# Prompt values stored by pairs of heads, and sample queries loaded once and copied on chip, in a hybrid encoder step

## The chip, the cores and the metric

The kernel runs on one core of a Trainium2 chip. The metric is device time in microseconds of one execution. Before the change it is 3593.35 us (median of 3 runs, 3592.12 to 3600.36).

## What is computed

One inference step of a hybrid encoder with two layers, in float32. There are 1024 prompt rows of one new stream and 8 running streams with 16 new frames each (128 sample rows), 1152 rows of width 1024 in all. Layer 0 mixes by two kinds of attention side by side: A, a sliding window, and B, differential attention with 4 heads (8 query and key heads of 64, 4 value heads of 128). Layer 1 mixes by C, a forgetting attention with 16 heads of 64. Each mixer is followed by a SwiGLU feed-forward of inner width 2816. The sample streams attend to caches of 2048 past rows each. Cut to what bears on the change:

```
qa, ka, va, qb, kb, vb = split(h @ w_in)              # layer 0: one projection for A and B
B:  p = softmax(q2 k2^T * scale, chunk mask)          # two score maps per head
    o = (p[:, 0] - lam * p[:, 1]) @ v                 # v: 4 heads of 128
C:  s = q k^T * scale + cq - ck, causal               # 16 heads of 64
    o = softmax(s) @ v
samples: the same with k, v = concat(cache (8, 2048, ...), the 16 new frames)
```

## The kernel before

The program is a row of stages, each with a barrier at its end: the first projection (`project_ab`, names abp_), A's attention for the prompt (pa_) and the samples (sa_), the joint attention of B (jb_), output projection (abm_), feed-forward (f_), the C projection (`project_c`, c_), the joint attention of C (jc_), output projection (cm_) and feed-forward again. All DMAs are issued by SyncE (SPq in the trace), in program order, on one queue.

The two projections go by pieces of output columns and, within a piece, by tiles of 128 rows. For each such step TensorE sums a product in PSUM, ScalarE copies it to one of two SBUF buffers z, and SyncE stores z to HBM: values go once to the kernel's output and once to an internal tensor (`v_ab`, `v_c`) that is laid out by rows, [1152 rows, width]. ScalarE may write z again two steps later, when its stores have landed (line 300 and line 614). The C projection cuts its 1024 value columns at 344 and 692.

The joint attention (`joint_attention`) works on the prompt and on the samples at the same time. It runs over units, one for each head of the prompt: 8 in jb, 16 in jc. A unit has 8 steps, one for each tile of 128 prompt queries, in the order 3, 4, 2, 5, 1, 6, 0, 7. Each engine has its program written out by hand, step by step, and they meet at semaphores. In a step n TensorE computes the scores of step n + 3 (lines 1489 to 1491), transposes the probabilities of n + 1 (line 1500) and, in every other step, multiplies them by the values (line 1517), or turns the last output back (line 1532). ScalarE computes the exponential of step n + 2 (line 1694), copies the output ahead of the turn back (line 1703) and copies transposed probabilities to SBUF (line 1659). VectorE takes the maxima and transposes the cache keys.

In the same unit one sample stream (and in jc one half of the heads) is worked off: its keys (`kc`, 4 MB, two buffers) are transposed, key scores are computed in step 7 (lines 1544 and 1552) out of four row groups of 32 partitions, and in the next unit ScalarE copies those scores (line 1714, step 0), exponentiates them (line 1727, steps 2 and 3) and TensorE multiplies by the cache values (`vc`, line 1607, steps 4 and 5). For this the queries of the samples must stand in each of the four row groups. One load, at lines 1371 to 1377, brings the queries of four units: SyncE issues four DMAs of the same 128 KB, one to each group of 32 partitions. It comes before unit 0 and then a unit ahead of units 4, 8 and 12 (4 in jb). VectorE waits for it in step 4 of the unit (line 1814) and spreads the unit's queries into `q_blocks` (line 1819).

The prompt's values are loaded per pair of heads (`load_v`, line 1322): 1024 rows by 128 columns to [128 partitions, 8 tiles, 128]. The source is laid out by rows, so each partition receives 8 separate pieces of 512 B. At a stage's start the order of SyncE is: planes of head 0 (`load_qk`), values of pair 0, keys of unit 0, queries, some small tensors, planes of head 1, values of pair 1, and then the loop at line 1395.

Of the kernel before, what the change touches and what calls it, by code (L numbers as in the profile page):

```python
# [25 lines left out]
P = 128  # L26
D = 1024
# [80 lines left out]
def project_ab(nc, name, x_tile, gain, w, tables, q_hi, q_lo, q_sample, v, k_rows_out, v_rows_out, direct):  # L108
# [14 lines left out]
    with Stage(nc, name) as st:  # L123
# [31 lines left out]
        def value_stores(s):  # L155
            c, t = steps[s]
            if AB_TURNED[c] == AB_PIECES[c][1]:
                return []
            src = z[:, s % 2, AB_TURNED[c]:AB_PIECES[c][1]]
            at = 0 if c == 0 else P  # L160
            return [(v[t * P:(t + 1) * P, at:at + AB_PIECES[c][1] - AB_TURNED[c]], src)] + v_rows_out(c, t, src)
# [285 lines left out]
def project_c(nc, name, ht_hi, ht_lo, w, bias, cache, q_hi, q_lo, q_sample, v, k_out, v_out, logf_prompt, logf_sample, ck, neg_c):  # L447
# [21 lines left out]
    with Stage(nc, name) as st:  # L469
# [29 lines left out]
        def row_stores(s):  # L499
            c, kind, t = steps[s]  # L500
            first, n, _ = C_PIECES[c]
            token = slice(t * P, (t + 1) * P)
            if kind == "k":
                return [(k_out(t)[:, first - D:first - D + n], z[:, s % 2, 0:n])]
            n = n_v if kind == "f" else n
            part = slice(first - 2 * D, first - 2 * D + n)
            return [(v[token, part], z[:, s % 2, 0:n]), (v_out(t)[:, part], z[:, s % 2, 0:n])]
# [644 lines left out]
def joint_attention(nc, name, groups, planes, k_first, v, v_cols, dv, q_sample, q_first, k_cache, v_cache, k_new, v_new,  # L1152
# [80 lines left out]
    with Stage(nc, name) as st:  # L1233
# [36 lines left out]
        out_ops = 1 if diff else 2  # L1270
# [34 lines left out]
        def _(sp):  # L1305
# [16 lines left out]
            def load_v(p):  # L1322
                if p >= 2:
                    sp.wait_ge(pv_done, S * (p - 1))
                c = v_cols(2 * p)
                sp.dma_start(vp[:, p % 2], v[0:PROMPT, c:c + P].rearrange("(t p) d -> p t d", p=P)).then_inc(
                    v_loaded[p % 2], 16)
# [43 lines left out]
            def load_q(g):  # L1371
                if g >= 1:
                    sp.wait_ge(q_done, 8 * g)
                first, streams = q_first + g // 2 * width, slice(g % 2 * P // 2, (g % 2 + 1) * P // 2)
                for a in range(4):
                    sp.dma_start(q_all[Q * a:Q * a + Q], q_sample[first:first + width, streams].rearrange(
                        "(j p) n -> p j n", p=Q)).then_inc(q_loaded, 16)
# [306 lines left out]
        def _(act):  # L1684
# [31 lines left out]

            def copy_new_scores(u):
# [19 lines left out]
            for u in range(U + 1):  # L1737
                for s in range(S):
# [22 lines left out]
                    if u >= 1 and s == 5:  # L1761
                        copy_probs(act, u - 1, 4)
                    if u < U and s == 5:
# [4 lines left out]
        def _(dve):  # L1768
# [43 lines left out]
            def blocks(u):  # L1812
                if u % 4 == 0:
                    dve.wait_ge(q_loaded, 64 * (u // 4 + 1))
# [937 lines left out]
def build(nc, a, out):  # L2752
# [3 lines left out]
    v_c = nc.dram_tensor("v_c", (TOKENS, D), F32, kind="Internal").ap()  # L2756
    planes_ab = nc.dram_tensor("planes_ab", (2, 13 * P, PROMPT), F32, kind="Internal").ap()
# [55 lines left out]
    project_ab(nc, "abp", x0, gain(0, 0), a["w_ab_in"][0], a["rope_table"], planes_ab[0], planes_ab[1], qs_ab, v_ab, k_rows_out, v_rows_out, direct)  # L2813
# [5 lines left out]
    joint_attention(nc, "jb", 1, planes_ab, D + P, v_ab, lambda h: P + h // 2 * P, P, qs_ab, 512,  # L2819
                    by_stream(a["cache_b_k"]), by_stream(a["cache_b_v"]), flat(out["b_k_sample"]), v_ab[samples, P:],  # L2820
                    o_ab, A_Q * DH, row_odd=a["odd_heads"], b_lambda=a["b_lambda"][0])
    with Stage(nc, "m0") as st:
# [6 lines left out]
        project_c(nc, "c", ht_hi, ht_lo, a["w_c_in"][0], a["c_forget_bias"], a["cache_c_logf"][0], planes_c[0], planes_c[1], qs_c, v_c,  # L2829
# [3 lines left out]
    joint_attention(nc, "jc", 2, planes_c, D, v_c, lambda h: h * DH, DH, qs_c, 0, by_stream(a["cache_c_k"]),  # L2833
# [40 lines left out]
```

## Time and profile before

| What | Value |
|---|---|
| Median of 3 runs | 3593.35 us |
| Profiled execution | 3596.04 us |
| Its span, first to last instruction | 3594.3 us |
| TensorE busy (matmul) | 3327.7 us, 93% |
| VectorE, ScalarE, GpSimd busy | 1598.0, 1124.3, 254.9 us |
| Mean granted TensorE clock | 0.966 |
| DMA | 493.16 MB, 398381 packets, 137 GB/s over the span |
| jb, from its first load to its last product | about 414 to 704 us |
| jc, the same | about 2055 to 2600 us |

The page's second part cuts the span into 40 slices. TensorE is at 9 tenths in most of them. The DMA engines are at 9 tenths in slices 6 and 7 (jb) and 24 to 29 (jc) and at 1 to 5 tenths nearly everywhere else, the feed-forwards at 1. The feed-forwards take most of the time and are not touched. So the stretches to look at are the two joint attentions, and the stores of the two projections.

### The profile page before, as it was taken

The numbers are of one execution on the slowest core, as the hardware profiler recorded it, in microseconds if no ns is written. First come the engines' busy times: TensorE is split into PE (matmuls) and PEld (weight loads), VectorE is DVE, ScalarE is ACT, GpSimd is POOL, SyncE is SP. The second block draws the span as 40 slices with busy tenths as digits, with TensorE's granted clock in tenths as the row PEclk, the third lists the DMA queues.
The fourth block names the chain that finished last, engine by engine and source line by source line (L and its number), as shares of the span: only waits on it lengthen the run. The fifth ranks groups of instructions, "written<-read, shape, count | busy, mean of one in ns | idle before, by whom it ended". The sixth has DMA issues, their size and how long they took to land. (4 is left out here: it accounts for less than half of the span.)

```text
span 3594.3 us, 62088 instructions
## 1 busy us (share of the span) xinstructions
PE 3327.7 (93%) x24520; PEld 2908.6 (81%) x24520; DVE 1598.0 (44%) x2913; ACT 1124.3 (31%) x2343; POOL 254.9 (7%) x338
## 2 busy tenths in 40 slices
PE   7997699798999999998799889999798999999997
PEld 7886477587999999997689866767577999999996
DVE  5427477463333333335331167777543333333334
ACT  4215355443212112112322155556433211121111
POOL 2310000032000000003000000000022000000003
PEclk9998799899999999999899999999999999999999
DMA  5436499533111111112554399999543111111112
GB/s 172 125 125 189 148 373 333 178 138 117 35 35 58 35 47 35 35 47 71 153 167 145 104 348 357 341 335 342 197 172 117 35 35 48 45 47 35 35 38 97
DMA packets 398381, 493.16 MB, mean 137 GB/s; under 512 B 68464, under 2 KB 250256, under 8 KB 398032
## 3 DMA queue, kind: packets, MB, share of 16 engines
q1 hardware_dynamic: 398176, 490.35, 41.2%
q8 instruction: 138, 2.26, 0.3%
q14 instruction: 67, 0.55, 0.0%
HBM read 407.10 MB, written 84.10 MB: 137 GB/s over the span
## 5 line engine op out<-in xcount | busy, mean ns | idle before, releaser
L2561 DVE TENSOR_TENSOR f_gated<-f_gated,f_up 128x384 f32<-128x384 f32 x132 | 73.1, 554 | 734.9 <-ACT f_gated L2491 734.9
L2585 DVE TENSOR_TENSOR f_y<-f_y,f_down 128x512 f32<-128x512 f32 x396 | 269.7, 687 | 229.4 <-PE f_down L2680 229.3
L2667 PE MATMUL f_gate<-m_ht_hi,f_w_hi 128*128 128x384 f32 x1056 | 355.0, 336 | 12.1 <-DVE f_w_lo L2612 12.1
L2667 PE MATMUL f_gate<-m_ht_lo,f_w_hi 128*128 128x384 f32 x1056 | 354.4, 336 | 0.0
L2667 PE MATMUL f_gate<-m_ht_hi,f_w_lo 128*128 128x384 f32 x1056 | 354.4, 336 | 0.0
L2667 PE MATMUL f_up<-m_ht_hi,f_w_lo 128*128 128x384 f32 x1056 | 352.7, 334 | 0.0
L2667 PE MATMUL f_up<-m_ht_hi,f_w_hi 128*128 128x384 f32 x1056 | 352.7, 334 | 0.0
L2667 PE MATMUL f_up<-m_ht_lo,f_w_hi 128*128 128x384 f32 x1056 | 352.7, 334 | 0.0
L2680 PE MATMUL f_down<-f_wo_hi,f_act_hi 128*128 128x512 f32 x792 | 313.4, 396 | 10.6 <-DVE f_y L2585 9.3
L2680 PE MATMUL f_down<-f_wo_hi,f_act_lo 128*128 128x512 f32 x792 | 309.9, 391 | 0.0
L2680 PE MATMUL f_down<-f_wo_lo,f_act_hi 128*128 128x512 f32 x792 | 309.6, 391 | 0.0
L2491 ACT ACTIVATE f_gated<-f_gate 128x384 f32<-128x384 f32 x132 | 65.0, 493 | 684.5 <-PE f_up L2667 684.3
L2667 PEld LDWEIGHTS f_gate<-m_ht_hi,f_w_hi 128*128 128x128 f32 x1056 | 199.5, 189 | 13.6 <-issue 12.8
L2667 PEld LDWEIGHTS f_gate<-m_ht_lo,f_w_hi 128*128 128x128 f32 x1056 | 199.5, 189 | 0.8
L2667 PEld LDWEIGHTS f_gate<-m_ht_hi,f_w_lo 128*128 128x128 f32 x1056 | 199.4, 189 | 0.0
L2667 PEld LDWEIGHTS f_up<-m_ht_hi,f_w_hi 128*128 128x128 f32 x1056 | 198.2, 188 | 0.0
L2667 PEld LDWEIGHTS f_up<-m_ht_lo,f_w_hi 128*128 128x128 f32 x1056 | 198.2, 188 | 0.0
L2667 PEld LDWEIGHTS f_up<-m_ht_hi,f_w_lo 128*128 128x128 f32 x1056 | 198.2, 188 | 0.0
L2680 PEld LDWEIGHTS f_down<-f_wo_hi,f_act_hi 128*128 128x128 f32 x792 | 149.5, 189 | 52.7 <-DVE f_y L2585 19.0
L1828 DVE STREAM_TRANSPOSE jc_kc<-jc_kc 128x512 f32<-128x512 f32 x256 | 180.8, 706 | 14.2
L2680 PEld LDWEIGHTS f_down<-f_wo_hi,f_act_lo 128*128 128x128 f32 x792 | 149.2, 188 | 31.8
L2680 PEld LDWEIGHTS f_down<-f_wo_lo,f_act_hi 128*128 128x128 f32 x792 | 149.5, 189 | 29.9
(404 smaller groups left out, 6756.6 us busy)
## 6 DMA issues: line engine op xcount, KB each, us to landing
jc_kc<-in_cache_c_k SPq DMA_DIRECT2D x64, 1024.0 KB, 11.1
jc_vc<-in_cache_c_v SPq DMA_DIRECT2D x64, 1024.0 KB, 10.3
jb_kc<-in_cache_b_k SPq DMA_DIRECT2D x32, 1024.0 KB, 11.7
jb_vc<-in_cache_b_v SPq DMA_DIRECT2D x32, 1024.0 KB, 8.6
m_raw<-in_w_ffn_in SPq DMA_DIRECT2D x44, 512.0 KB
f_raw<-in_w_ffn_in SPq DMA_DIRECT2D x44, 512.0 KB
f_raw_o<-in_w_ffn_out SPq DMA_DIRECT2D x22, 1024.0 KB, 6.2
m_raw<-x SPq DMA_DIRECT2D x18, 512.0 KB, 4.1
```

Of the source, the lines that this page charges most:

```text
L1828: dve.transpose(kc[:, u % 2, t, :], kc[:, u % 2, t + 1, :]).then_inc(kt_done, 1)
L2491: act.activation(silu[:, b], gate[:, q, 0:gw], ACT.Silu).then_inc(silu_done, 1)
L2561: dve.tensor_tensor(prod[:, b], silu[:, b], up[:, q, 0:gw], ALU.mult).then_inc(prod_done, 1)
L2585: dve.tensor_tensor(part, part, down[:, half, :], ALU.add).then_inc(added, 1)
L2667: last = pe.matmul(acc[:, q, 0:gw], a[:, s, k, u, :], b[:, k, token], start=(k == 0 and j == 0), stop=(k == KT - 1 and j == 2))
L2680: last = pe.matmul(down[:, half, :], a[:, s, t * P:(t + 1) * P], b[:, s, half * 512:(half + 1) * 512], start=(n == 0), stop=(n == 5))
```

## The change

Prompt values are also laid out by pairs: two new internal tensors, [pairs, 128 partitions, 8 tiles, 128], so that one load reads 4 KB in a row for each partition. In the first projection the store of B's prompt values goes there instead of to `v_ab`. In the C projection it goes there in place of `v_c`, cut where a pair of heads ends (at every 128 columns): the pieces of 344, 348 and 332 columns give 2, 3 and 2 stores. Sample rows still go to `v_ab` and `v_c`, and the stores to the kernel's outputs stay as they are.

The queries are loaded by one DMA, to partitions 0 to 31, and ScalarE copies them three times, to partitions 32, 64 and 96. These copies, with their wait for the load, stand in ScalarE's program in step 1 of units 0, 4, 8 and 12 (0 and 4 in jb), behind that step's copy of transposed probabilities. VectorE waits in step 4 for the three copies.

```diff
@@ project_ab, value_stores
             src = z[:, s % 2, AB_TURNED[c]:AB_PIECES[c][1]]
+            if AB_PIECES[c][0] == VB and t < TILES_P:
+                return [(v_pairs[:, :, t].rearrange("h p d -> p h d"), src.rearrange("p (h d) -> p h d", d=P))] + v_rows_out(c, t, src)
             at = 0 if c == 0 else P
@@ project_c, row_stores
-            return [(v[token, part], z[:, s % 2, 0:n]), (v_out(t)[:, part], z[:, s % 2, 0:n])]
+            out = [(v_out(t)[:, part], z[:, s % 2, 0:n])]
+            if t == TILES_P:
+                return [(v[token, part], z[:, s % 2, 0:n])] + out
+            stores, a = [], part.start
+            while a < part.stop:
+                heads = max(1, (part.stop - a) // P) if a % P == 0 else 1
+                b = min(a - a % P + heads * P, part.stop)
+                src = z[:, s % 2, a - part.start:b - part.start].rearrange("p (h d) -> p h d", h=heads)
+                stores.append((v_pairs[a // P:a // P + heads, :, t, a % P:a % P + (b - a) // heads].rearrange("h p d -> p h d"), src))
+                a = b
+            return stores + out
@@ joint_attention, SyncE
-                c = v_cols(2 * p)
-                sp.dma_start(vp[:, p % 2], v[0:PROMPT, c:c + P].rearrange("(t p) d -> p t d", p=P)).then_inc(
-                    v_loaded[p % 2], 16)
+                sp.dma_start(vp[:, p % 2], v_pairs[p]).then_inc(v_loaded[p % 2], 16)
-                for a in range(4):
-                    sp.dma_start(q_all[Q * a:Q * a + Q], q_sample[first:first + width, streams].rearrange(
-                        "(j p) n -> p j n", p=Q)).then_inc(q_loaded, 16)
+                sp.dma_start(q_all[0:Q], q_sample[first:first + width, streams].rearrange("(j p) n -> p j n", p=Q)).then_inc(q_loaded, 16)
@@ joint_attention, ScalarE
+            def copy_queries(g):
+                act.wait_ge(q_loaded, 16 * (g + 1))
+                for a in range(1, 4):
+                    act.activation(q_all[Q * a:Q * a + Q], q_all[0:Q], ACT.Copy).then_inc(q_copied, 1)
                     if u >= 1 and s == 5:
                         copy_probs(act, u - 1, 4)
+                    if u < U and u % 4 == 0 and s == 1:
+                        copy_queries(u // 4)
@@ joint_attention, VectorE
-                    dve.wait_ge(q_loaded, 64 * (u // 4 + 1))
+                    dve.wait_ge(q_copied, 3 * (u // 4 + 1))
@@ build
+    v_pairs_ab, v_pairs_c = (nc.dram_tensor(n, (heads, P, TILES_P, P), F32, kind="Internal").ap()
+                             for n, heads in (("v_pairs_ab", B_H), ("v_pairs_c", C_H // 2)))
```

## Rows read from the trace of the kernel before

**Rows 1.** Windows: stretch, us, busy us per engine (x instructions), PEclk, DMA, GB/s.

```profile
2110.00:2560.00 450.00, 429.08 (x6520) 314.39 (x6516) 328.58 (x741) 269.04 (x660) 0.00 (x0) 1.00 0.97 339
```

**Rows 2.** Waits, 413 to 703: who waited, releaser, total us, times, longest.

```profile
PE jb_scores_a L1489 <- DMA jb_q_lo<-planes_ab: 14.6, 2, 11.2
```

**Rows 3.** Timeline, jc opening: start us, us, engine, operation, [idle before, releaser].

```profile
2066.69 9.94 SPq L1376 DMA_DIRECT2D jc_q_all<-qs_c  x4
...
2073.55 0.50 ACT L1659 ACTIVATE jc_probs_t<-jc_turned 128x384 f32<-128x384 f32 x1
...
2074.55 0.39 ACT L1703 ACTIVATE jc_o_turn<-jc_pv 128x256 f32<-128x256 f32 x1
...
2076.09 0.56 PE L1532 MATMUL jc_pv<-jc_halves,jc_o_turn 128*128 128x64 f32 x4
...
2086.53 0.62 SPq L1320 DMA_DIRECT2D jc_k_hi<-ck  x1
...
2090.92 0.79 PE L1489 MATMUL jc_scores_a<-jc_k_both,jc_q_hi 128*128 128x512 f32 x1 [8.63 <-DMA jc_k_hi<-ck]
```

**Rows 4.** Windows, jc opening.

```profile
2077.00:2080.00 3.00, 1.56 (x15) 1.08 (x14) 2.83 (x8) 1.69 (x6) 0.00 (x0) 1.00 1.29 187
...
2081.00:2084.50 3.50, 1.29 (x13) 1.15 (x11) 0.00 (x0) 0.98 (x2) 0.00 (x0) 1.00 0.17 37
...
2091.00:2096.00 5.00, 5.00 (x54) 3.73 (x54) 4.27 (x9) 1.15 (x4) 0.00 (x0) 0.50 1.06 376
```

**Rows 5.** Timeline, jb opening.

```profile
427.01 7.48 SPq L1376 DMA_DIRECT2D jb_q_all<-qs_ab  x4
...
431.96 0.38 ACT L1703 ACTIVATE jb_o_turn<-jb_pv 128x256 f32<-128x256 f32 x1 [0.76 <-PE jb_pv L1517]
```

**Rows 6.** ScalarE groups by form: operation, shapes, count, busy us, mean ns.

```profile
L2482 ACT ACTIVATE f_w_hi<-m_raw 128x2048 fp32r<-128x2048 f32 x20 | 38.0, 1900 | 0.0
...
L1727 ACT ACTIVATE jc_s_scores<-jc_s_scores,jc_s_neg 128x1024 f32<-128x1024 f32 x16 | 18.4, 1150 | 1.7 <-DVE jc_s_neg L1849 1.7
```

**Rows 7.** Timeline, jc, the unit that uses the third query load.

```profile
2333.78 0.43 ACT L1703 ACTIVATE jc_o_turn<-jc_pv 128x256 f32<-128x256 f32 x1
...
2334.85 0.87 ACT L1659 ACTIVATE jc_probs_t<-jc_turned 128x512 f32<-128x512 f32 x2 [0.64 <-PE jc_turned L1500]
...
2334.81 0.56 PE L1532 MATMUL jc_pv<-jc_halves,jc_o_turn 128*128 128x64 f32 x4
...
2340.90 0.66 PE L1532 MATMUL jc_pv<-jc_halves,jc_o_turn 128*128 128x64 f32 x4 [0.61 <-ACT jc_o_turn L1703]
```

**Rows 8.** Line 1544, four per unit, four windows: ns, first and last start.

```profile
L1544 PEld LDWEIGHTS jc_turned<-jc_bias,jc_select x64: 181/182/184, 2101.0 to 2573.4; 32*128 32x128 f32 x64
...
L1544 PEld LDWEIGHTS jc_turned<-jc_bias,jc_select x12: 181/182/184, 2194.6 to 2260.1; 32*128 32x128 f32 x12
...
L1544 PEld LDWEIGHTS jc_turned<-jc_bias,jc_select x12: 181/182/184, 2260.0 to 2321.4; 32*128 32x128 f32 x12
...
L1544 PEld LDWEIGHTS jc_turned<-jc_bias,jc_select x8: 181/182/184, 2321.3 to 2355.3; 32*128 32x128 f32 x8
```

**Rows 9.** Windows, jc: inside a query load; ahead of two key scores.

```profile
2185.50:2191.50 6.00, 6.00 (x133) 4.76 (x127) 3.52 (x8) 2.57 (x9) 0.00 (x0) 1.00 1.08 173
...
2255.00:2261.00 6.00, 6.00 (x69) 4.21 (x59) 4.50 (x12) 3.35 (x8) 0.00 (x0) 1.00 0.68 222
...
2316.00:2322.00 6.00, 6.00 (x81) 4.53 (x70) 4.29 (x11) 3.37 (x9) 0.00 (x0) 1.00 0.92 323
```

**Rows 10.** Timeline, jc: inside the key scores of unit 7.

```profile
2326.76 0.58 PE L1552 MATMUL jc_s_ps<-jc_kc,jc_q_blocks 32*32 32x512 f32 x1 [1.16 <-issue]
```

**Rows 11.** The C projection: timeline of SyncE, then waits.

```profile
1735.82 12.18 SPq L560 DMA_DIRECT2D c_zeros<-in_cache_c_logf  x8
...
PE c_acc L753 <- ACT c_z L619: 4.5, 1, 4.5
...
SPq L566 <- ACT c_z L619: 103.6, 41, 4.8
```

More of the change, by code:

```diff
@@ L105, with project_ab @@
 AB_KEYS = (KA, KB)
-def project_ab(nc, name, x_tile, gain, w, tables, q_hi, q_lo, q_sample, v, k_rows_out, v_rows_out, direct):
+def project_ab(nc, name, x_tile, gain, w, tables, q_hi, q_lo, q_sample, v, v_pairs, k_rows_out, v_rows_out, direct):
     slots = 3
@@ L444, with project_c @@
             (0, 512, "q"), (512, 512, "q"))
-def project_c(nc, name, ht_hi, ht_lo, w, bias, cache, q_hi, q_lo, q_sample, v, k_out, v_out, logf_prompt, logf_sample, ck, neg_c):
+def project_c(nc, name, ht_hi, ht_lo, w, bias, cache, q_hi, q_lo, q_sample, v, v_pairs, k_out, v_out, logf_prompt, logf_sample, ck, neg_c):
     gw = TOKENS // 3
@@ L1149, in strided, with joint_attention @@
     return bass.AP(ap.tensor, ap.offset + offset, [list(ap.ap[0])] + [list(d) for d in dims])
-def joint_attention(nc, name, groups, planes, k_first, v, v_cols, dv, q_sample, q_first, k_cache, v_cache, k_new, v_new,
+def joint_attention(nc, name, groups, planes, k_first, v_pairs, dv, q_sample, q_first, k_cache, v_cache, k_new, v_new,
                     o, o_first, ck=None, neg_c=None, row_mask=None, selector=None, row_odd=None, b_lambda=None):
@@ L1269, in joint_attention @@
              "s_inv_done", "s_pv_done", "scaled", "ot_done", "ot_copied", "s_stored"))
-        out_ops = 1 if diff else 2
+        out_ops, q_copied = 1 if diff else 2, st.sem("q_copied")
         emptied_sem = {"act": act_emptied, "dve": dve_emptied}
@@ L2811, in v_rows_out @@
         return new_frames("a_v_sample", src) if t == TILES_P else []
-    project_ab(nc, "abp", x0, gain(0, 0), a["w_ab_in"][0], a["rope_table"], planes_ab[0], planes_ab[1], qs_ab, v_ab, k_rows_out, v_rows_out, direct)
+    project_ab(nc, "abp", x0, gain(0, 0), a["w_ab_in"][0], a["rope_table"], planes_ab[0], planes_ab[1], qs_ab, v_ab, v_pairs_ab, k_rows_out, v_rows_out, direct)
     prompt_attention(nc, "pa", A_Q // 2, lambda i, e: (2 * i + e) * DH, lambda i, e: D + (i // 2) * DH,
@@ L2818, in build @@
                   v_ab[samples, 0:P], a["a_sinks"], o_ab)
-    joint_attention(nc, "jb", 1, planes_ab, D + P, v_ab, lambda h: P + h // 2 * P, P, qs_ab, 512,
+    joint_attention(nc, "jb", 1, planes_ab, D + P, v_pairs_ab, P, qs_ab, 512,
                     by_stream(a["cache_b_k"]), by_stream(a["cache_b_v"]), flat(out["b_k_sample"]), v_ab[samples, P:],
@@ L2828, in build @@
                      lambda t: x2[t * P:(t + 1) * P], gain_next=gain(1, 0))
-        project_c(nc, "c", ht_hi, ht_lo, a["w_c_in"][0], a["c_forget_bias"], a["cache_c_logf"][0], planes_c[0], planes_c[1], qs_c, v_c,
+        project_c(nc, "c", ht_hi, ht_lo, a["w_c_in"][0], a["c_forget_bias"], a["cache_c_logf"][0], planes_c[0], planes_c[1], qs_c, v_c, v_pairs_c,
                   tile_of(flat(out["c_k_prompt"]), flat(out["c_k_sample"])),
@@ L2832, in build @@
                   out["c_logf_sample"][0].rearrange("s f h -> (s f) h"), ck, neg_c)
-    joint_attention(nc, "jc", 2, planes_c, D, v_c, lambda h: h * DH, DH, qs_c, 0, by_stream(a["cache_c_k"]),
+    joint_attention(nc, "jc", 2, planes_c, D, v_pairs_c, DH, qs_c, 0, by_stream(a["cache_c_k"]),
                     by_stream(a["cache_c_v"]), flat(out["c_k_sample"]), v_c[samples], o_c, 0, ck=ck, neg_c=neg_c,
```

## The prediction

> **What bounds the kernel now.** I read the page's busy shares and slices first, then the table of windows by stage, then the waits and timelines of the two joint attentions (jb for layer 0, jc for layer 1), the only stages that the new loads and copies touch. In the middle of jc TensorE is busy 429 of 450 us and the DMA engines are at 0.97 [rows 1]: two limits side by side, with ScalarE at 60%. TensorE is hardly ever seen waiting for data there. The times at which the key scores open tell more: 472.3 us over 15 units, 31.5 each, against 30.65 in the two units that no query load touches (2260.0 to 2321.3) [rows 8]. So 472.3 - 15 x 30.65 = 12.5 us is all that the steady part of jc could give back without a shorter instruction list. Both openings do wait for DMA: TensorE stands 8.63 us before head 1 in jc [rows 3], and in jb 14.6 - 11.2 = 3.4 us [rows 2].
>
> **The change, part by part.**
>
> (a) *Queries loaded once.* A load today is four issues of 128 KB in pieces of 64 numbers (256 B): 2048 pieces, tomorrow 512. In jc's opening the four hold SyncE 9.94 us [rows 3], the DMA engines move 187 GB/s while they drain, then 37 GB/s, because SyncE had been held and reaches the second head's planes late [rows 4]. The last of those is issued at 2086.53 and TensorE restarts at 2090.92 [rows 3]. Three quarters of the query bytes gone and SyncE free some 7.5 us earlier puts head 1 in SBUF by about 2083, ahead of need, so this stall goes. What is late next is (b).
>
> (b) *The wait moves to ScalarE, and three steps earlier.* Today VectorE waits for the queries in step 4 of unit 0. Now ScalarE waits for them in step 1, behind the copy at 2073.55 [rows 3]. The queries are queued behind the 4 MB of keys, which drain until about 2077 (the low-bandwidth stretch begins there [rows 4]). With the cheaper value load ahead I put the landing at 2078. Then three copies, each 32 partitions x 1024 numbers. The trace has no such instruction: half of a 128 x 2048 copy is 0.95 us, an exponential of 128 x 1024 is 1.15 [rows 6], so 2.85 to 3.45 for three; I take 3.0, nearer to the copy. Queued behind them on ScalarE are the exponential of step 2 and the copy of the first output, done today at 2074.94 [rows 3]; it would be done at 2078 + 3.0 + 0.5 + 0.4 = 2081.9. TensorE's turn-back waits for it, and everything that ScalarE empties after. The turn-back starts today at 2076.09 [rows 3], so it shifts 5.8 us, and the work that ends today where the stall begins, at 2090.92 - 8.63 = 2082.3, ends at 2088.1. Against 2090.92 that is 2.8 us won of the 8.6. TensorE's clock row reads 0.50 (1.2 GHz) in the five us after the old stall [rows 4]; a pause of 5.8 us in place of 8.6 may bring the same fall, but over work that is paced by ScalarE. I take 3.5 us won in jc's opening; the ends are 8 won (the stall goes and the copies lie beside it) and 1 lost.
>
> In jb the same sum is worse, since only 3.4 us of stall are there to trade. SyncE's four held issues end at 434.49 [rows 5], a sign of when the keys ahead have drained, and I take 434.8 for the landing. The output copy, at 431.96 + 0.38 today [rows 5], would end at 434.8 + 3.0 + 0.9 = 438.7, 6.4 us later. TensorE comes late for that copy anyway, in jc by 1.2 us (2076.09 against 2074.94); of that I count 0.7, which leaves 5.7. TensorE reaches head 1 some 2.3 us later than today. Its half clock after the old stall may move ahead of the restart as well. I take 0.5 lost, ends 4 lost and 3 won. Both openings together: 3.0 won.
>
> (c) *Copies in the running pipeline.* Four more groups of queries come in mid-stream: jb's second, jc's second to fourth. Their loads are issued a unit ahead, so ScalarE finds the data there. But step 1 lies in its densest stretch: in jc's unit 8 the output copy starts at 2333.78 and ends 0.6 us before TensorE uses it (2334.81), one gap of 0.64 us follows, and then ScalarE runs without a break until TensorE waits 0.61 us for it at 2340.90 [rows 7]. So 3.0 us put in front of 2333.78 are covered for about 0.7 and delay TensorE by 2.3. Four times: 9.2 us lost. Ends: 4 x 0.7 = 3 if TensorE's instruction gaps swallow part, 4 x 3.4 = 14 if nothing covers.
>
> (d) *DMA time given back.* Inside a query load the DMA engines move 173 GB/s [rows 9] against 339 in the whole stretch [rows 1], so 512 KB and what is between it take 5 to 7 us in place of about 1.5. TensorE doesn't wait for these bytes. What I see instead: in the 6 us ahead of the key scores the DMA share is 0.68 in a clean unit and 0.92 in the unit after a query load [rows 9], and inside that unit's key scores TensorE stands 1.16 us for "issue", that is for no semaphore [rows 10]. The units at the two loads take 65.4 us for two and 33.9 for one, against 30.65: 4.1 and 3.25 us over [rows 8]. I read that as instructions fetched late through DMA engines that have lost their pause. If the loads shrink to a quarter, most of the 12.5 us should come back; I take 9 in jc and 0.5 in jb, ends 0 and 13. The Trainium skill speaks against this reading: "Runtime: NRT & Kernel Launch", section on instruction fetch mechanics, calls the crossing of a 16 KiB block mostly hidden. By that rule nothing comes back here and the sum would be 9.5 us higher; the 1.16 us row stands against it, and I make the case a rival.
>
> (e) *Values by pairs.* Each load of 512 KB goes from 1024 pieces of 512 B to 128 of 4 KB. It is never waited for in either stage after the opening. Its saving is part of (a) and (d).
>
> (f) *The stores.* In the first projection one store of 256 KB becomes one of four times the pieces, beside matmuls that leave SyncE idle between steps: nothing. In the C projection prompt rows are stored in 2, 2 and 3 pieces where there was 1 (the pieces are cut at 344 and 692): 32 more issues of about 0.35 us on SyncE. They matter only at the start, where SyncE is held 12.18 us by the cache loads and TensorE already waits 4.5 us for ScalarE's z, whose buffer waits for its stores [rows 11]. Two steps' stores, one issue more each: 0.7 us lost, ends 0 and 2. If SyncE's idle time in the later steps were gone, 24 issues x 0.35 = 8 us would be the price; but it waits 103.6 us for z in 41 steps, 2.5 in each [rows 11], and the extra stores take at most 0.7 of them.
>
> **Sum** against the profiled execution, 3596.04 us (span 3594.3): -3.0 + 9.2 - 9.5 + 0.7 = -2.6, so 3593.4. That execution lies 2.7 us above the median of the runs, 3593.35; against the median the forecast is 3591 us. Copies on ScalarE and DMA time given back nearly cancel. A measurement of this kernel can tell about 0.3% (10.8 us) from no change.
>
> **The rivals.**
>
> *Relief that is hidden anyway.* The issue gaps have another cause and stay. For it: TensorE has waits of "issue" in clean units too. Against: they are longest after query loads. Then -3.0 + 9.2 + 0.7 = +6.9 over the median: 3600.
>
> *ScalarE's wait decides (slower).* The openings win nothing, because ScalarE stands behind 4 MB of keys in both, and each mid-stream group costs its full copies. Price: openings 4 lost, 4 x 3.0 = 12, C projection 0.7, 3 returned by DMA: +14, so 3607. It decides once the queries land later than about 2081 in jc. For it: [rows 7]; against: TensorE has nothing to do but wait from 2082 today. The Trainium skill's advice to issue a DMA early and wait late ("DMA: Bandwidth & Descriptors", rules for kernel authors) points the same way, as the change waits earlier.
>
> *The transfers are the bound (faster).* The DMA engines, at 0.97, set jc's pace more than TensorE's rows show. Everything of the 12.5 comes back, the openings give 8 in jc and 1 in jb, and the copies cost 4 x 1.5 = 6 since a unit freed of late data has room: -12.5 - 9 + 6 + 0.7 = -15, so 3578.
>
> **How the numbers follow.** Forecast (near-cancelling, 3585 to 3597) 0.48; hidden relief 0.20; ScalarE decides 0.14; transfers decide 0.18. Faster by over 0.3% is most of the last and a little of the first: 0.17. Slower is most of ScalarE's case: 0.13. Same: 0.70. The ends of the terms added in full would be -29 and +21; eight in ten I put between 3577 and 3607.
>
> **What would show it.** In the changed profile: 18 ScalarE copies of about 1.0 us from the query tile, and six query issues in place of 24; in jc's opening a ScalarE wait of about 4 us for the queries and no TensorE wait for the head's planes, key scores of unit 0 opening near 2097.5 (today 2101.0 [rows 8]); units without a query load still at 30.6 us, those with copies near 32 to 33, issue gaps in key scores mostly gone. Wrong would be: a ScalarE copy far from 1 us, units at 30.6 with copies in them (ScalarE had room), or clean units that get shorter (DMA was the bound).

## Result: 3615.73 us, 0.5% slower

| | before | after |
|---|---|---|
| Median of 10 runs each | 3594.42 us (3591.24 to 3604.80) | 3615.73 us (3610.15 to 3618.81) |
| Ratio, 95% interval | 1 | 1.0050 (1.0040 to 1.0061) |
| Span of the profiled execution | 3594.3 us | 3613.7 us |

The forecast was 3591, its range ended at 3607. The change costs 21 us, and the 19.4 us by which the two spans differ lie almost wholly in jb and jc. "Opening" is from a stage's first instruction to the first key score of its first unit, "steady" from there to the key scores of its last unit, "tail" the rest; all are read from starts and ends in the traces:

| us | before | after | difference |
|---|---|---|---|
| jb opening / steady / tail | 41.9 / 222.4 / 23.7 | 47.0 / 226.2 / 25.2 | +5.1 / +3.8 / +1.5 |
| jc opening / steady / tail | 46.9 / 472.3 / 23.7 | 49.3 / 478.8 / 25.9 | +2.4 / +6.5 / +2.2 |
| C projection | 324.3 | 325.1 | +0.8 |

The remaining -2.9 us are in stages that the change doesn't touch, or hardly. The tails are chance as far as the traces tell: over the seventeen of this study they lie between 22.3 and 25.9 us in jb and jc, with copies and without. An "issue gap" is a stop of TensorE for which the profile shows no semaphore.

In the steady part of jc the three units that hold copies take 34.1, 34.1 and 35.6 us. In the profile of before the same units took 33.0, 33.9 and 33.3, but issue gaps had made them slow; in a second profile of that kernel (e11, below) they took 30.6, 30.6 and 32.1. Against that one, each group costs 3.5 us. Unit 0 loses another 3.6 (34.3 us against 30.7) to an issue gap of 2.1 us and a fall of the clock behind it. This seems to come with the change, though no step of the prediction has it: the gap stands in nine of the ten kernels that load a stage's first queries once (not in e8), with unit 0 at 33.4 to 34.3 us, and in none of the four with an unshifted list that load them four times (before, e1, e7, e11), with unit 0 at 30.6 to 30.7. Why it comes is not shown, nor that it moves the medians: e8 without it and e9 with it are alike there.

**The middle of jc.** A window of the changed kernel, shifted by the 9.1 us by which its jc starts later; columns as in [rows 1]:

```profile
2119.00:2569.00 450.00, 426.75 (x6473) 312.97 (x6471) 323.07 (x729) 273.02 (x654) 0.00 (x0) 0.98 0.92 328
```

Against [rows 1] the DMA share fell from 0.97 to 0.92, as the change meant. But the trace holds 47 matmuls less in the same 450 us, and its mean clock is 0.98 in place of 1.00. The transfers were relieved and the stage got slower. That they weren't its limit is shown by e7 below, which takes bytes away and changes nothing else.

**The opening of jc.** Timeline of the changed kernel, the rows that answer to [rows 3]:

```profile
2075.88 2.43 SPq L1385 DMA_DIRECT2D jc_q_all<-qs_c  x1
...
2081.64 0.50 ACT L1667 ACTIVATE jc_probs_t<-jc_turned 128x384 f32<-128x384 f32 x1
...
2087.31 0.61 SPq L1332 DMA_DIRECT2D jc_k_hi<-ck  x1
...
2090.39 3.21 ACT L1728 ACTIVATE jc_q_all<-jc_q_all 32x1024 f32<-32x1024 f32 x3 [8.25 <-DMA jc_q_all<-qs_c]
2093.62 0.47 ACT L1702 ACTIVATE jc_probs<-jc_scores_a,jc_neg_top 128x256 f32<-128x256 f32 x1
...
2094.09 0.37 ACT L1711 ACTIVATE jc_o_turn<-jc_pv 128x256 f32<-128x256 f32 x1
...
2094.51 1.11 PE L1540 MATMUL jc_pv<-jc_halves,jc_o_turn 128*128 128x64 f32 x4 [10.18 <-ACT jc_o_turn L1711]
```

ScalarE has nothing to do from 2082.1 to 2090.4: it stands in front of the first copy until the queries land. Three copies take 3.21 us. The exponential and the output copy behind them were wanted at 2084, and TensorE stands 10.18 us. The stall before head 1 [rows 3] is gone; in its place is a longer one, beginning 20.1 us behind the stage's start where the old one began at 27.2. SyncE did what was expected of it: head 1's last plane is issued at 2087.31, in the clock of before 2078.2, 8.3 us earlier.

**The opening of jb**, the same, to be held against [rows 2, 5]:

```profile
433.29 3.21 ACT L1728 ACTIVATE jb_q_all<-jb_q_all 32x1024 f32<-32x1024 f32 x3 [6.46 <-DMA jb_q_all<-qs_ab]
...
437.42 0.69 PE L1537 MATMUL jb_pv<-jb_ident,jb_o_turn 128*128 128x128 f32 x2 [7.86 <-ACT jb_o_turn L1711]
```

**A group in mid-stream.** Timeline, then two windows just before and behind TensorE's restart; they answer to [rows 7]:

```profile
2209.75 0.38 ACT L1711 ACTIVATE jc_o_turn<-jc_pv 128x256 f32<-128x256 f32 x1
2215.15 1.09 ACT L1722 ACTIVATE jc_s_scores<-jc_turned 128x512 f32<-128x512 f32 x2 [5.02 <-PE jc_turned L1560]
...
2219.70 3.21 ACT L1728 ACTIVATE jc_q_all<-jc_q_all 32x1024 f32<-32x1024 f32 x3
...
2223.83 0.66 PE L1540 MATMUL jc_pv<-jc_halves,jc_o_turn 128*128 128x64 f32 x4 [2.67 <-ACT jc_o_turn L1711]
```

```profile
2222.50:2225.60 3.10, 1.64 (x14) 1.34 (x15) 1.08 (x4) 3.07 (x9) 0.00 (x0) 1.00 1.05 390
2225.80:2229.00 3.20, 3.20 (x17) 2.74 (x15) 1.49 (x4) 2.91 (x7) 0.00 (x0) 0.50 1.05 387
```

TensorE waits 2.67 us where it waited 0.61, and right behind that pause its granted clock reads 0.50 (1.2 GHz) for one stretch of 3.41 us, with no further pause in it. All four mid-stream groups show both (2.67 us three times in jc, 2.25 in jb). In the kernel before no stretch at 1.2 GHz lies between the first and the last key scores of either stage. Note also the second row: 4.5 us ahead of the copies ScalarE had been idle for 5.02 us. The waits of the stage, before and then after:

```profile
PE jc_pv L1532 <- ACT jc_o_turn L1703: 9.0, 15, 0.6
PE jc_s_ps L1552 <- issue: 4.6, 4, 1.7
```

```profile
PE jc_pv L1540 <- ACT jc_o_turn L1711: 15.2, 15, 2.7
PE jc_s_ps L1560 <- issue: 2.6, 3, 1.1
PE jc_s_ps L1597 <- issue: 2.1, 1, 2.1
```

### The profile page after: what moved, and what is told of

Its sections match the earlier page's. It is cut to its first block and busy times, and to the rows that moved or that the text cites. A ratio compares the mean times of both kernels' runs of the same rounds, so it can differ in the third digit from the quotient of the medians.

```text
span 3613.7 us, 62120 instructions
## 1 busy us (share of the span) xinstructions
PE 3335.1 (92%) x24520; PEld 2914.5 (81%) x24520; DVE 1598.1 (44%) x2913; ACT 1143.6 (32%) x2361; POOL 254.5 (7%) x338
```

## The experiments

Theory A after the traces: ScalarE's place decides, by its wait for the queries in the openings and by its copies in mid-stream with the half clock behind each. Rivals: the values' larger pieces make other loads late (B), the opening alone (D) or the mid-stream alone (E) decides. Ratios are to the kernel before, run alongside.

**e1_values_only, e2_queries_only.** The change in its two halves. e1 is the changed kernel with `load_q` and VectorE's wait as before; e2 the kernel before with

```
-for a in range(4): sp.dma_start(q_all[Q * a:Q * a + Q], ...)
+sp.dma_start(q_all[0:Q], ...)
+copy_queries(u // 4)          # ScalarE, step 1 of each fourth unit
```

> Only the values part of the change: stored and loaded by pairs of heads; each group of queries is loaded four times, as before. Theory A (ScalarE's work and wait is what costs: openings +7.4 us, copies in mid-stream, and the half clock that follows each pause) expects the whole loss to be gone: 3590 to 3597 us, openings of jb and jc at 42 and 47 us from the stage's start to the first key score, 3.41 us half-clock stretches in mid-stream gone. Rival B (the values' 4 KB pieces crowd out the keys' and queries' pieces on the DMA engines, so that these land later) expects openings still 3 to 7 us longer than before and 3600 to 3608 us. Rival C (DMA time given back is real): a few us below before, 3585 to 3590.

> Only the queries part: loaded once, copied by ScalarE in step 1; values stored and loaded as before. Theory A expects all of the loss or a little more, 3613 to 3620 us: ScalarE waits 6 to 8 us for the first queries in each opening, TensorE 2.7 us at each mid-stream copy. Rival B expects less than half of the loss, 3596 to 3605, with the queries landing some us earlier than in the changed kernel.

e1: 3595.15, ratio 0.9998 (0.9989 to 1.0006); openings 40.8 and 47.4. e2: 3614.89, ratio 1.0048 (1.0036 to 1.0060). The queries' part is the whole loss; the values' part costs and wins nothing, to within 4 us. B falls.

**e3_first_only.** The changed kernel; groups after each stage's first are loaded four times:

```
 def load_q(g):
+    if g == 0: one load, return
+    for a in range(4): four loads
-if u < U and u % 4 == 0 and s == 1:
+if u == 0 and s == 1:
     copy_queries(u // 4)
```

> The changed kernel, but only the first group of queries of each stage is loaded once and copied by ScalarE; the later groups (one in jb, three in jc) are loaded four times. It splits the loss. Theory A by the trace: the openings' 7.4 us stay, and most of the slower units' 10.3 us (3.8 in jb, 6.5 in jc) go: 3604 to 3608 us, with no TensorE wait of 2.7 us and no half-clock stretch in mid-stream except those that unit 0 itself brings. Rival D (the opening alone decides, since a late start leaves the load queue late through the whole stage): 3611 to 3616, with slow units all the same. Rival E (mid-stream copies decide): 3594 to 3600.

3606.63, ratio 1.0026 (1.0015 to 1.0037): half the loss is back. Openings 46.4 and 49.3 as in the changed kernel, and no TensorE wait for ScalarE of 2.67 us in mid-stream. D and E fall: there are two losses, by the ratios 9.3 us at the first groups and 8.6 at the later ones, the second net of what one load in place of four gives.

**e4_on_gpsimd.** The copies on an idle engine:

```
+for g in range(U // 4):                      # GpSimd
+    pool.wait_ge(q_loaded, 16 * (g + 1))
+    for a in range(1, 4):
        ...                                   # wait for its own copy before
        pool.tensor_copy(q_all[Q * a:Q * a + Q], q_all[0:Q]).then_inc(q_copied, 1)
-copy_queries(u // 4)                         # ScalarE
```

> The changed kernel with the 18 copies on GpSimd, idle in the middle of both stages, each group as soon as its load has landed; ScalarE waits for nothing new. Theory A expects both losses gone: openings at 42 and 47 us or less, 3588 to 3597 us. If GpSimd's copies take far longer than ScalarE's 1.05 us (3 us each would still fit before VectorE's step 4 of unit 0 in jc only just), VectorE and then TensorE wait in the openings: 3597 to 3604. Rival F (the loss is not ScalarE's but the late landing of a single query load): VectorE's wait at step 4 moves the openings as now, 3605 to 3615.

3591.91, ratio 0.9987 (0.9979 to 0.9996). Openings 38.7 and 43.5, 3.2 and 3.4 us shorter than before the change. Two rows of its timeline:

```profile
2077.82 3.22 POOL L1474 COPY jc_q_all<-jc_q_all 32x1024 f32<-32x1024 f32 x3 [19.04 <-DMA jc_q_all<-qs_c]
...
2083.05 0.79 PE L1504 MATMUL jc_scores_a<-jc_k_both,jc_q_hi 128*128 128x512 f32 x1 [4.64 <-DMA jc_k_hi<-ck]
```

The queries land 26.0 us behind jc's start (2051.8), as late as in the changed kernel (26.2), and now nobody but GpSimd waits. The stall before head 1 is 4.64 us in place of 8.63: the relief of step (a), seen by itself. The last rival of the expectation falls.

**e5_queries_first.** The wait taken away by an earlier load, the copies left in step 1:

```
 load_qk(0)
+load_q(0)
 load_v(0)
 load_keys(0)
-load_q(0)
```

> The changed kernel with the first query load issued by SyncE right after head 0's planes, ahead of the values and the 4 MB of keys; ScalarE still makes the three copies in step 1, and the mid-stream copies stay. If the wait is what costs in the openings (theory A), ScalarE waits for nothing there, what is left is 3.2 us of copies: the openings (stage start to the first key score of the first unit) come out near 32 us in jb and 37 in jc, against 36.6 and 40.1 in the changed kernel and 28.4 and 34.0 with the copies on GpSimd; 3605 to 3610 us in all. If the copies themselves cost as much as the wait, the openings stay within 2 us of the changed kernel's: 3612 to 3617. The keys land 0.5 us later at most.

3605.58, ratio 1.0023 (1.0013 to 1.0034), 10 us better than the changed kernel. Openings 39.6 and 43.0, level with GpSimd's 38.7 and 43.5. (The expectation's numbers for openings end at TensorE's first use of the query blocks, for the new keys; in that reading e5 has 29.1 and 33.8.) Timeline, jc:

```profile
2078.00 3.22 ACT L1728 ACTIVATE jc_q_all<-jc_q_all 32x1024 f32<-32x1024 f32 x3
...
2082.13 0.66 PE L1540 MATMUL jc_pv<-jc_halves,jc_o_turn 128*128 128x64 f32 x4 [1.95 <-ACT jc_o_turn L1711]
...
2090.58 0.50 PE L1497 MATMUL jc_scores_a<-jc_k_both,jc_q_hi 128*128 128x512 f32 x1 [3.48 <-DMA jc_k_hi<-ck]
```

No idle time ahead of the copies. They still hold TensorE 1.95 us, but head 1's planes are late anyway (3.48 us), so in jc's opening the copies are nearly free and only the wait was dear (43.0 against 43.5 with GpSimd's copies; 39.6 against 38.7 in jb).

**e6_first_and_split.** As e5, one copy in each of steps 1, 2 and 3: `if u % 4 == 0 and s in (1, 2, 3): copy_queries(u // 4, s)`.

> As the kernel with the first queries loaded first, and the three copies of every group spread over steps 1, 2 and 3, one in each. If what costs in mid-stream is one pause of 2.7 us and the 3.41 us at 1.2 GHz that follow it, three delays of 1.07 us, each half covered by slack of 0.6 to 0.7 us in ScalarE's row, leave TensorE waits of at most 1.1 us, no half clock in mid-stream, and units with copies at 31 to 32 us: 3593 to 3600 us. If ScalarE's total work is what costs, all of 3.2 us per group stays: 3602 to 3608.

3600.94, ratio 1.0014 (1.0005 to 1.0023): between the two expectations, and the reason of neither holds. The copy in step 1 is nearly covered (TensorE waits 0.51 us), those in front of the step-2 output are not (2.19 us), and the fall of the clock followed in three of the four groups. In jc the copy unit without the fall takes 2.9 us more than in e9 below (33.5 against 30.6), the two with it 4.5 and 4.1 more. Cutting the copies up only spreads them over a stretch in which ScalarE has too little slack for them.

**e7_no_later_queries.** The kernel before without `load_q` for every group after a stage's first: it leaves out reading the later queries and uses the first ones again.

> The kernel before without the query loads after the first group of each stage (jb's second, jc's second to fourth): it leaves out reading these queries, and uses the first ones again. It measures step (d) of the prediction by itself, in full: what the stream would win if no query byte moved in it. If the issue gaps come from DMA engines that the query loads keep busy: 9 to 12.5 us in jc, 3584 to 3588 us, and TensorE's waits of over 1 us for no semaphore, 177 us and 399 us behind jc's start, gone. If they have another cause (hidden relief): 3592 to 3596 us, and the same waits at the same places of the instruction list.

3594.08, ratio 0.9997 (0.9988 to 1.0007). The rival "hidden relief" holds: all later query bytes together are worth 1 us by the ratio, at most 4 by its interval. The issue gaps are still there. A row of the kernel before, then one of e7:

```profile
2233.39 0.58 PE L1552 MATMUL jc_s_ps<-jc_kc,jc_q_blocks 32*32 32x512 f32 x1 [1.29 <-issue]
```

```profile
2225.84 0.58 PE L1550 MATMUL jc_s_ps<-jc_kc,jc_q_blocks 32*32 32x512 f32 x1 [1.56 <-issue]
```

Counted in matmuls and weight loads from jc's first, both are at the 4269th.

**e8_gpsimd_first.** e4 with e5's order of loads.

> The kernel with the copies on GpSimd, and the first query load issued ahead of the values and keys. With the copies on GpSimd the queries are needed only by VectorE in step 4, and TensorE waited 1.31 us for the query blocks in jb's opening and nothing in jc's. Theory A: at most 1.3 us better than the 3592 of that kernel, 3588 to 3593. Rival (keys come later by what the 512 small pieces take, and the planes of head 1 with them): 3592 to 3596.

3590.52, ratio 0.9984 (0.9975 to 0.9993): the best of the study, not to be told from e4.

**e9_in_idle.** e5 with the mid-stream copies one step earlier, still on ScalarE, still in one piece:

```
+if 4 <= u < U and u % 4 == 0 and s == 0:
+    copy_queries(u // 4)
 if u >= 1 and s == 0:
     copy_scores(u - 1, 0)      # waits for TensorE's key scores
```

> The kernel with the first queries loaded first, and the mid-stream copies on ScalarE one step earlier: in step 0, right ahead of the copy of the key scores, where ScalarE stands idle 5.0 us in every unit waiting for TensorE. The same three copies by the same engine, 3.2 us in one piece, nothing else changed. If where they stand decides (theory A), the 15 us between e5_queries_first (3605.6) and e8_gpsimd_first (3590.5) come back, with no TensorE wait of 2.67 us and no half clock in mid-stream: 3589 to 3594. If the loss is in having them on ScalarE at all, or in the writes to the query tile while TensorE and VectorE run: 3600 to 3606.

3590.74, ratio 0.9987 (0.9978 to 0.9996). Timeline and the stage's waits:

```profile
2193.57 3.22 ACT L1728 ACTIVATE jc_q_all<-jc_q_all 32x1024 f32<-32x1024 f32 x3
2198.56 0.60 ACT L1722 ACTIVATE jc_s_scores<-jc_turned 128x512 f32<-128x512 f32 x1 [1.77 <-PE jc_turned L1560]
```

```profile
PE jc_pv L1540 <- ACT jc_o_turn L1711: 9.0, 15, 0.6
```

The idle time of 5.02 us has become 3.22 of copies and 1.77 of idle time, and TensorE's waits for ScalarE are back at 9.0 us, as before the change. The same work one step earlier is worth 15 us by the medians. In the traces the four units with copies take 3.5, 3.3, 3.0 (jc) and 3.3 us (jb) less than in e5, 13.1 together. In jc 2.0 of each is TensorE's shorter wait; the other 1.0 to 1.5 us are matmuls that no longer run at 1.2 GHz. That is the price of one fall, a little under half of its 3.41 us.

**e10_two_copies.** e5 with two copies in place of three in the mid-stream groups (`for a in range(1, 4 if g == 0 else 3)`): it leaves out the fourth row group's new queries.

> The kernel with the first queries loaded first and copies in step 1, with two copies instead of three in the four mid-stream groups: the fourth row group keeps old queries, which leaves out part of the computation. It separates the clock from the wait. TensorE's wait falls by one copy, 1.05 us, from 2.67 to 1.6 us. If the wait alone costs, 4 x 1.05 = 4.2 us are won over e5_queries_first's 3605.6: 3601 to 3602. If the shorter pause no longer brings the 3.41 us stretch at 1.2 GHz (half of 3.41 us each), 4 x 2.75 = 11 us: 3594 to 3595. If some of the stretches stay, in between.

3597.31, ratio 1.0004 (0.9995 to 1.0012), 8.3 us below e5 by the medians and 6.8 by the ratios, each of which is known to about 3 us only; the waits alone would give 4.2. Timeline, then windows behind the three pauses in jc:

```profile
2209.03 0.66 PE L1540 MATMUL jc_pv<-jc_halves,jc_o_turn 128*128 128x64 f32 x4 [1.59 <-ACT jc_o_turn L1711]
```

```profile
2209.20:2213.00 3.80, 3.66 (x32) 3.07 (x33) 2.76 (x7) 3.80 (x9) 0.00 (x0) 1.00 1.05 388
2335.60:2339.00 3.40, 3.26 (x30) 2.73 (x30) 2.77 (x7) 3.40 (x7) 0.00 (x0) 1.00 1.05 388
2463.90:2467.00 3.10, 3.10 (x18) 1.87 (x17) 2.81 (x7) 3.10 (x6) 0.00 (x0) 0.50 1.04 384
```

After a pause of 1.59 us the clock stayed up twice in jc and also in jb (1.17 us there), and fell once. The medians alone would not part the clock from the wait, the units do: against e5 the two of jc where it stayed up are 1.9 and 1.8 us shorter and jb's 2.7, the one where it fell 1.2, about the missing copy's 1.05. The fall is a cost of its own.

**e12_planes_up.** e8 with `load_qk(1)` right behind `load_keys(0)`.

> The kernel with GpSimd's copies and the first queries loaded first, and head 1's planes issued right behind the keys, ahead of the frame mask, the head rows, the bias and the new keys, whose issue holds SyncE some 9 us. TensorE's stall for these planes in jc's opening was 8.63 us before the change and 2.96 with GpSimd's copies. If SyncE's held issue is what makes them late, the stall goes, with part of the 10.2 us at 1.2 GHz behind it: 3 to 6 us won, 3585 to 3588. If the keys' 4 MB decide, the planes land as now: 3589 to 3592. If bias or new keys become late for the first key scores: 3592 to 3598.

3596.81, ratio 1.0002 (0.9993 to 1.0011): 6 us worse than e8, as the last of the three outcomes had it. The stall before head 1 went only from 2.96 to 2.30 us, and VectorE now waits 6.2 us for the new keys, whose issue has moved behind the planes; TensorE waits for VectorE's blocks in turn. Waits, 2078 to 2099:

```profile
DVE jc_turned_new L1849 <- DMA jc_new<-out_c_k_sample: 6.2, 1, 6.2
PE jc_turned L1584 <- DVE jc_q_blocks L1834: 5.7, 1, 5.7
```

**e11_shifted_list, e13_shift_by_matmuls, e14_shift_250, e15_shift_64.** What the issue gaps are: the kernel before, with instructions added at the head of TensorE's list in jc. One run each.

```
+pe.nop()                                                       # e11: 128 times
+pe.wait_ge(setup, 5)                                           # e13, e14, e15
+pe.matmul(scores_a[:, 0:P], ident_b[:], mask[:], ...)          # e13: 64 times
+pe.matmul(scores_a[:, 0:16], ident_b[:], mask[:, 0:16], ...)   # e14: 125, e15: 32 times
```

> The kernel before with 128 empty instructions at the head of TensorE's list in jc, where it waits for its first planes anyway. It asks what the issue gaps of step (d) are. In four kernels with four different amounts of query traffic TensorE stood 1.1 to 1.8 us for no semaphore 174 to 180 us and 394 to 400 us behind jc's start, always in the key scores. If these are places of the instruction list (its fetch), all move to earlier lines by 128 instructions, some 4 to 5 us, out of or to another part of the key scores, and other gaps move as well. If they are times at which the DMA engines are busiest, or belong to the key scores' own work, they stay at the same lines and times.

> The kernel before with 64 small matmuls at the head of TensorE's list in jc, from about 2057 on, while it waits for its first planes (their result is overwritten): 128 instructions, and these are executed ones, since the 128 empty instructions of e11_shifted_list left no mark in the trace and were perhaps never in the program. The question is the same. If the issue gaps of over 0.7 us in the key scores are places of the instruction list, they move 128 instructions ahead: those that stood at the 4269th, 8007th and 10747th TensorE instruction of jc in all kernels stand at the same count with the new ones counted, that is on other work. If they belong to this work, they stay on it, at the 4397th, 8135th and 10875th. In time no change that one run can tell: 3590 to 3602.

> The kernel before with 125 small matmuls (250 TensorE instructions) at the head of jc's list. In e13_shift_by_matmuls (128 instructions) the issue gaps left their places: counted with the new instructions they stand at 2528, 3527, 5268, 6266, 9006, 10004, 11745, which is again 249 times a whole number apart from each other, and the steady part took 486.4 us (475 to 481 in the kernels with the same stream and no ScalarE copies in step 1). If TensorE's list comes in blocks of some 249 matmuls and weight loads, a shift by 250 puts the same work at the block ends again: gaps of over 0.7 us at 1530, 4269, 8007 and 10747 plus 250, the steady part back at 475 to 481 us. If e13's gaps were this one run's luck, the gaps stand anywhere else.

> The same with 32 matmuls, 64 instructions. By blocks of 249: the gaps stand at places that are a multiple of 249 (within 3) behind 1530, counted with the new instructions, and on other work than before; the steady part somewhere between 475 and 490 us. If not blocks: gaps at 1594, 4333, 8071 and 10811, on the same work as before.

e11 (3590.83) decides nothing on its question: its page counts 62088 instructions, as before the change, so the empty ones are not among those that ran. It is a second profile of the kernel before instead, and as that it is worth much: its steady part of jc takes 466.3 us, not 472.3 (first and last starts 2102.1 and 2568.4 against [rows 8]):

```profile
L1548 PEld LDWEIGHTS jc_turned<-jc_bias,jc_select x64: 181/182/184, 2102.1 to 2568.4; 32*128 32x128 f32 x64
```

e13, e14 and e15 took 3604.20, 3605.54 and 3602.68 us beside 3605.06 for the kernel before, no difference that one run tells. The executed instructions did move the gaps. Places of TensorE's waits of over 0.4 us for no semaphore, from the 1000th to the 14000th matmul or weight load of jc, added ones counted (in brackets the us):

| kernel | places |
|---|---|
| before | 1530 (0.46), 3767 (0.46), 4017 (1.59), 4269 (1.29), 7009 (1.16), 7503 (1.05), 8007 (0.43), 9498 (0.49), 10747 (1.69) |
| e11 (the same program) | 1530 (0.46), 4269 (1.56), 8007 (0.97), 9498 (0.49), 10747 (0.87) |
| e7 | 1530 (0.73), 4269 (1.56), 7009 (0.61), 7503 (1.32), 8007 (0.70), 10747 (1.15) |
| e4 | 1027 (1.71), 1530 (0.67), 4269 (1.56), 8007 (0.97), 9498 (0.49), 10747 (1.15) |
| e13 (128 added) | 2528 (1.59), 3023 (0.88), 3527 (1.40), 5268 (0.89), 6266 (0.74), 9006 (1.54), 10004 (0.76), 11745 (0.66), 12242 (2.12), 12744 (0.74) |
| e14 (250 added) | 1283 (1.30), 4525 (1.63), 7265 (1.40), 7759 (0.84), 8263 (0.64), 9754 (0.49), 10501 (1.53), 11003 (1.45) |
| e15 (64 added) | 2024 (0.75), 2528 (0.70), 5268 (1.14), 8007 (1.86), 9006 (0.57), 11243 (1.70), 11745 (0.48) |

(4017 stands behind a wait for ScalarE that had ended 0.57 us before.) The distances between them are multiples of 249.2 to within 7 (4269 - 1530 = 2739, eleven times 249.0; 3527 - 2528 = 999, four times 249.8). e13 and e15 share four places though their work is shifted by another amount, and e14's are those of before and e4 plus 256 (all but 10501), on work six instructions away. So a gap belongs to a place in the list. Most show inside the key scores, where a matmul or weight load starts every few hundredths of a us:

```profile
2169.75 0.61 PE L1557 MATMUL jc_s_ps<-jc_kc,jc_q_blocks 32*32 32x512 f32 x2 [1.59 <-issue]
```

```profile
2237.84 0.58 PE L1557 MATMUL jc_turned<-jc_kc,jc_q_blocks 32*32 32x512 f32 x1 [1.63 <-issue]
```

(e13's 2528th and e14's 4525th.)

The traces also hold what ends these stops. On the page of before a queue of its own carries instructions, 138 packets of 16384 bytes; the second line is the window 2231.0 to 2231.1 us, which holds one of them:

```profile
q8 instruction: 138, 2.26, 0.3%
q8 instruction: 1, 0.02, 68.4%
```

That packet starts at 2231.01 and takes 1.1 us, and TensorE goes on at 2233.39 (the row in e7's section), 2.4 us behind its start. Over all seventeen traces, in the same part of jc, each of the 102 stops of over 0.4 us for no semaphore ends 2.3 to 2.8 us behind the start of such a packet. Of the 248 stops that a semaphore ended, 4 do (4017 is one); the others end anywhere from 0.3 to 12 us behind one. So TensorE stands at these places for a block of instructions that comes late. Why a block is late at one crossing and not at the next is not shown.

The Trainium skill, "Runtime: NRT & Kernel Launch", section on instruction fetch mechanics, gives blocks of 256 instructions; with the waits that lie between the matmuls the 249 fit it, while "mostly hidden" holds only for most of the crossings: these show 0.4 to 2.1 us each. e14 contradicts its own expectation in one point: its steady part took 475.6 us, not the 466 to 472 of this measure in the unshifted kernels, with a gap at 10501 that has no counterpart in the unshifted kernels. One execution each does not tell what an alignment is worth.

## Why the prediction was wrong

Medians: 3615.7 - 3591 = 24.7 us too low. Point by point, by its own steps:

**(a) SyncE free earlier: right.** 8.3 us earlier against 7.5 foretold. With the copies out of ScalarE's way (e4, e8) the two openings are 6.6 and 5.6 us shorter together than before the change; "the stall goes" was too much, 4.64 and 2.96 us of it stay there.

**(b) The wait moved to ScalarE: the step that failed first.** The landing was put at 2078 in jc, since the keys were thought to drain until 2077, where a stretch of low bandwidth begins [rows 4]. It came at 2090.39 - 9.1 = 2081.3, just beyond the point of 2081 that the text itself gave for "ScalarE's wait decides". In jb it was 436.4 in the clock of before, against 434.8. The trace of before had the answer: of the keys' last load in jc, issued at 2065.62, it says (1 MB, us to landing)

```profile
jc_kc<-in_cache_c_k SPq DMA_DIRECT2D x1, 1024.0 KB, 14.4
```

so the keys landed at 2080.0, and the DMA engines were at a share of 1.29 in that stretch of low bandwidth [rows 4], busy to the end. In the changed kernel the keys landed at 2080.5 in the clock of before, the queries right behind them.

Predicted for both openings -3.0, measured +7.5 in the traces. Of these 10.5 us, 3.3 and 1.6 are the later landings. Another 2.5 were never in the step's own sum: it gives 2.8 us won in jc and 2.3 lost in jb, and 3.5 won and 0.5 lost were taken, for a half clock that would cost less. It cost more: the clock reads 0.50 for 13.65 us in each changed opening, against 10.24 before in jc and 6.83 in jb. And TensorE now waits 1.4 us in jc and 1.6 in jb for VectorE's query blocks, since VectorE gets the queries after ScalarE; the prediction had nothing for this, and in the kernel before there is no such wait. e5 shows that it is the wait: with the data there, the same three copies in the same place leave the openings within 1 us of GpSimd's. Their price, 3.21 against 3.0, was right.

**(c) Copies in mid-stream: the mechanism right, the term too small.** TensorE waits 2.67 - 0.61 = 2.06 us more per group in jc (2.3 foretold). What was left out is the half clock behind the pause: half of 3.41 is 1.7 us. 2.06 + 1.7 = 3.8, four times 15; e5 against e8 and e9 measures 15.1 and 14.8. The units in the traces say a little less, 3.0 to 3.5 each. The prediction did weigh the clock in the openings and forgot it here.

**(d) DMA time given back: wrong.** 9.5 us were foretold; e7, with no later query byte at all, returns 1.1 (loses 2.5 to wins 4.3). Half of the reading of [rows 10] holds: the stop of 1.16 us ends 2.4 us behind the start of an instruction packet, so these were instructions fetched late. The other half, that the query loads make them late, fails: the gaps sit at places of the list whether or not queries are loaded, so "hidden relief" was the right case. By the Trainium skill's sentence that the step set against itself nothing comes back, and by e7 nothing did that shows. The 12.5 us over the clean units [rows 8] were partly the one execution profiled: e11 runs the same program 6 us faster through the same stretch. Traffic may add to single gaps; that is not shown, since e11, with all of the traffic, lacks the same four as e4 does (3767, 4017, 7009, 7503).

**(e), (f) Right.** Values by pairs: e1's 0.9998. C projection: +0.8 us in the trace against 0.7, but between the traces of kernels without the new stores the stage varies by over 2 us, so this shows only that nothing large was missed. Two slips of the text change nothing here: the pieces store in 2, 3 and 2 parts, not 2, 2 and 3, and the favourable ends of the terms add up to -21, not -29 (-8 - 3 + 3 - 13).

**What would have shown it.** Of the signs listed, the 18 copies of 1.05 us and the missing wait for the head's planes came; the ScalarE wait was 8.25 us, not 4, units with copies took 34.1 to 35.6 us in jc, not 32 to 33, and the issue gaps stayed. Not foreseen at all: the gap and the half clock in unit 0, 3.6 us in the trace.

Errors: (b) 10.5, (c) 5.8, (d) 8.4, together 24.7. Each is known to 2 or 3 us only, they mix single traces with medians, and unit 0's 3.6 us stand in none of them, so that the sum fits to the tenth is luck. They had one sign, which the near-cancelling sum had hidden. Of the rivals, "ScalarE's wait decides" had place and mechanism; its +14 lacked the clock and gave 3 us back to DMA.

**The version that beats both.** Queries loaded once, first group issued ahead of the keys, copies on GpSimd (e8, 0.9984) or in ScalarE's idle time (e9, 0.9987). Both intervals exclude 1, both gains, by the ratios 5.8 and 4.7 us, are below the 0.3% that the prediction took for the least that can be told.

## What to carry to other kernels

A copy is priced by where it stands in its engine's order, not by its length: the same 3.2 us cost nothing in ScalarE's idle time and 3.0 to 3.8 us of the stage's time one step later; look for the idle row of the engine before placing it. A wait moved to an engine that feeds TensorE must be checked against the landing of the load, and the landing of a load that stands last in the queue is to be read from the landings of those ahead of it, which the trace of before gives. The Trainium skill, "DMA: Bandwidth & Descriptors", rules for kernel authors, says to issue a DMA early and to wait for it late; e5 agrees, with 10 us for one moved line. Before crediting a change with the removal of small gaps, take a second profile of the same kernel, or leave the suspected cause out altogether and look whether they go.

## What the runs showed of the chip

- One pause of TensorE of 2.67 us, or 2.25, in a stretch otherwise at 2.4 GHz was followed each time (12 of 12 in the changed kernel, e2 and e5) by a stretch at 1.2 GHz, 3.41 us long in eleven and 6.83 in one; pauses of 1.17 and 1.59 us by one in 1 of 4 (e10), of 2.19 by one in 3 of 4 (e6). In e1 an issue gap of 1.05 us was enough, in e13 one of 2.12 was not, so the pause's length alone doesn't decide.
- ScalarE and GpSimd take the same time for a copy of 32 partitions x 1024 numbers: 3.21 and 3.22 us for three.
- Issue gaps of TensorE of over 0.4 us end 2.3 to 2.8 us behind the start of a 16384-byte instruction packet (102 of 102 in jc). They lie at places of its instruction list, multiples of 249 matmuls and weight loads apart, and differ in size between executions: at the 4269th 0.48 us in the changed kernel, 1.29 before, 1.56 in e11, which ran the same program as before, 1.83 in e8 and e9.
